# The sums of squares of four heads, taken by two reduced-form matmuls of a high and a low part

## The reference

```python
f = lbf + (1.0 - lbf) * jax.nn.sigmoid(fz)
log_f = jnp.log(f); k = 1.0 - f
o_hg = hgrn2_chunkwise(silu(q), log_f, k, i)       # per head: scores with decays, and a carried state
o_hg = rmsnorm(o_hg, hg_norm).reshape(B, T, HG_WIDTH) * jax.nn.silu(g)
o_cv = rmsnorm(gb * causal_dwconv3(gc * u), conv_norm)
return jnp.concatenate([o_hg, o_cv], axis=-1) @ w_out
```

## Time and profile before

| | us |
|---|---|
| median of 3 runs | 1118.38 |
| lowest, highest | 1118.32, 1120.45 |
| the profiled execution, its own time | 1120.16 |
| its span in the trace | 1118.2 |
| TensorE busy | 1106.8 |
| VectorE, ScalarE, GpSimd busy | 626.9, 522.2, 437.1 |

### The profile page before, as it was taken

The page is one execution under the profiler, slowest core; times in us unless marked ns, Lnnn a source line. Parts: engine busy times, 40 slices in busy tenths (PEclk is TensorE's granted clock), DMA queues, the critical chain, the costliest instruction groups (busy, mean ns, idle before and its releaser), DMA issues.

```text
span 1118.2 us, 17287 instructions
## 1 busy us (share of the span) xinstructions
PE 1106.8 (99%) x6358; PEld 971.0 (87%) x6358; DVE 626.9 (56%) x911; ACT 522.2 (47%) x725; POOL 437.1 (39%) x544
## 2 busy tenths in 40 slices
PE   9999999999999999999999999999999999999997
PEld 7889999988888888888888888888889999988886
DVE  6887777441222668888567123464787777440012
ACT  6545555542323555654466443354455555542221
POOL 0000000486665544434548883173000000485651
PEclk9999999999999999999999999999999999999999
DMA  7276775332323221222313442122187675332312
GB/s 240 76 210 188 194 197 169 114 112 96 113 94 111 77 76 57 76 76 76 113 57 133 163 157 76 39 81 102 45 226 188 178 197 169 114 113 96 112 57 76
DMA packets 48626, 135.33 MB, mean 121 GB/s; under 512 B 4672, under 2 KB 10944, under 8 KB 48448
## 3 DMA queue, kind: packets, MB, share of 16 engines
q1 hardware_dynamic: 43344, 118.38, 30.2%
q0 software_dynamic: 4032, 14.68, 7.7%
q10 hardware_dynamic: 1200, 1.57, 0.4%
HBM read 132.52 MB, written 2.10 MB: 120 GB/s over the span
## 4 chain that ended last, share of the span: by engine, by line
PE 53%; POOL 25%; issue 21%; DVE 0%; POOLq 0%; DMA 0%; ACT 0%; DVEq 0%; SPq 0%; ACTq 0%
POOL wl L438 25%; PE bank L1420 9%; PE bank L1422 9%; PE bank L1421 9%; PE bank L1522 4%; PE bank L1524 4%; PE bank L1523 4%; PE score L1523 3%; PE score L1522 3%; PE score L1524 3%; PE o_bank L1522 1%; PE o_bank L1524 1%; PE o_bank L1523 1%; PE bank L1479 1%; PE bank L1483 1%
## 5 line engine op out<-in xcount | busy, mean ns | idle before, releaser
L438 POOL TENSOR_TENSOR wl<-raw,wh 128x256 fp32r<-128x256 f32 x512 | 412.5, 839 | 326.0 <-ACT wh L472 281.8
L472 ACT ACTIVATE wh<-raw 128x1024 fp32r<-128x1024 f32 x124 | 130.1, 1054 | 162.2 <-PE bank L1422 158.1
L1420 PE MATMUL bank<-xh,wh 128*128 128x512 f32 x488 | 194.8, 399 | 0.0
L1422 PE MATMUL bank<-xh,wl 128*128 128x512 f32 x488 | 190.4, 390 | 0.0
L1421 PE MATMUL bank<-xl,wh 128*128 128x512 f32 x488 | 190.1, 390 | 0.0
L452 POOL DMA_DIRECT2D raw<-w_all x28 | 24.3, 869 | 330.1 <-DMA raw<-w_all 330.1
L1420 PE MATMUL bank<-zr,wh 128*128 128x512 f32 (+1 forms) x374 | 142.6, 381 | 0.0
L1422 PE MATMUL bank<-zr,wl 128*128 128x512 f32 (+1 forms) x374 | 141.7, 379 | 0.0
L1421 PE MATMUL bank<-zr,wh 128*128 128x512 f32 (+1 forms) x374 | 140.5, 376 | 0.0
L902 DVE SCALAR_TENSOR_TENSOR x<-bank,x 128x512 f32<-128x512 f32 (+1 forms) x31 | 21.3, 687 | 175.4 <-PE bank L1422 175.4
L1421 PEld LDWEIGHTS bank<-xl,wh 128*128 128x128 f32 x488 | 91.8, 188 | 19.9 <-issue 1.7
(11 more groups left out here) (304 smaller groups left out, 2493.8 us busy)
## 6 DMA issues: line engine op xcount, KB each, us to landing
raw<-w_all SPq DMA_DIRECT2D x200, 512.0 KB, 3.3
raw<-w_all POOLq DMA_DIRECT2D x28, 512.0 KB, 5.2
zf<-w_all SPq DMA_DIRECT2D x28, 256.0 KB, 4.5
x<-x_t SPq DMA_DIRECT2D x8, 256.0 KB, 6.2
out_t<-x SPq DMA_DIRECT2D x8, 256.0 KB, 2.4
raw<-w_all SPq DMA_DIRECT2D x6, 256.0 KB, 6.1
memf<-mem_t ACTq DMA_DIRECT2D x1, 1024.0 KB, 4.8
raw<-w_all ACTq DMA_DIRECT2D x2, 256.0 KB, 3.9
```

The costliest lines, as they stand in the source:

```text
L438: ins = nc.gpsimd.tensor_tensor(wl[:, slot, two], raw[:, slot, two], wh[:, slot, two].bitcast(f32), SUB)
L472: nc.scalar.activation(wh[:, slot, :], raw[:, slot, :], ACT.Copy).then_inc(hi_ready, 1)
L1420: nc.tensor.matmul(out_, a[0], b_[0], start=first, stop=False)
L1422: return nc.tensor.matmul(out_, a[1], b_[0], start=False, stop=last)
```

## The change

The matrix of ones gets a copy of type fp32r. In O, ScalarE copies osq to osq_h of type fp32r right after it made it. In each slot with an N step VectorE takes osq_l = osq - osq_h, as the first instruction of the slot, ahead of the eviction of the slot's projection. In N, TensorE waits for osq_lo instead of osq_ready, and for ones_ready, and makes two fp32r matmuls, ones_r by osq_h and ones_r by osq_l, into the same bank. osq_l lies in the memory of osq and osq_h in that of onrm: so osq_l is written in place, and osq_h only after the head before has released onrm (the wait for cat_lo).

```diff
--- before.py
+++ after.py
@@ -129,6 +129,7 @@
         convV, lf = ubuf[:, 0, :], ubuf[:, 1, :]
         half_tanh = gbuf[:, 0, :]
         ones = sb("ones", [128, 128])
+        ones_r = sb("ones_r", [128, 128], f32r)
         ident = sb("ident", [128, 128])
         masks = sb("masks", [128, MASK_COLS], u8)
         par = sb("par", [128, NPAR])
@@ -178,8 +179,12 @@
         kd = sb("kd", [128, T], f32, mix_mem)
         kdT = sb("kdT", [128, TT, 128], f32, mix_mem)
         S = sb("S", [128, NCH - 1, 128], f32, mix_mem)
-        osq = sb("osq", [128, T], f32, mix_mem)
-        onrm = sb("onrm", [128, T], f32, mix_mem)[:, :]
+        o_mem = ExitStack()
+        osq = sb("osq", [128, T], f32, o_mem)
+        onrm = sb("onrm", [128, T], f32, o_mem)[:, :]
+        o_mem.close()
+        osq_l = sb("osq_l", [128, T], f32r, mix_mem)
+        osq_h = sb("osq_h", [128, T], f32r, mix_mem)
         convC = sb("convC", [128, T], f32, mix_mem)
         convU = sb("convU", [128, 2 + T], f32, mix_mem)
         convO = sb("convO", [128, CC, T], f32, mix_mem)
@@ -289,6 +294,9 @@
         a22_loaded = [sem(f"a22_loaded{i}") for i in range(2)]
         x_old = sem("x_old")
         xn_new = sem("xn_new")
+        osq_hi = sem("osq_hi")
+        osq_lo = sem("osq_lo")
+        ones_ready = sem("ones_ready")
         xn_hi = sem("xn_hi")
         xn_lo = sem("xn_lo")
         t_new = sem("t_new")
@@ -730,6 +738,10 @@
                 if kind == "O":
                     act.wait_ge(o_done, h + 1)
                     nc.scalar.activation(osq[:, :], o_bank[:, :], ACT.Square).then_inc(osq_ready, 1)
+                    act.wait_ge(osq_ready, h + 1)
+                    if h > 0:
+                        act.wait_ge(cat_lo, h)
+                    nc.scalar.activation(osq_h[:, :], osq[:, :], ACT.Copy).then_inc(osq_hi, 1)
                 if kind == "N":
                     inverse_root(("N", h), osq[:, :], n_bank[:, :], 128)
                     act.wait_ge(cat_new, h + 1)
@@ -843,6 +855,8 @@
             V_ = nc.vector
             V_.memset(ones[:, :], 1.0).then_inc(consts_ready, 1)
             V_.memset(one, 1.0).then_inc(consts_ready, 1)
+            dve.wait_ge(consts_ready, 1)
+            V_.tensor_copy(ones_r[:, :], ones[:, :]).then_inc(ones_ready, 1)
             V_.memset(eps, EPS).then_inc(consts_ready, 1)
             link(V_.memset(acc[:, :], 0.0))
             V_.memset(rstd[:, :], 0.0).then_inc(group_read, 4)
@@ -1268,6 +1282,10 @@
                         .then_inc(cat_lo, 1)
 
             for at, (kind, c) in enumerate(MIX_SLOTS):
+                for step_kind, h, _ in STEPS[at]:
+                    if step_kind == "N":
+                        dve.wait_ge(osq_hi, h + 1)
+                        V_.tensor_tensor(osq_l[:, :], osq[:, :], osq_h[:, :].bitcast(f32), SUB).then_inc(osq_lo, 1)
                 g = SLOT_GROUP[at]
                 src = bank[g % 4][:, :]
                 if kind in "qfg":
@@ -1694,9 +1712,11 @@
                                                 start=False, stop=(c == NCH - 1), skip_group_check=True)
                     last.then_inc(o_done, 1)
                 if kind == "N":
-                    pe.wait_ge(osq_ready, h + 1)
+                    pe.wait_ge(osq_lo, h + 1)
                     n_wait(("N", h))
-                    nc.tensor.matmul(n_bank[:, :], ones[:, :], osq[:, :], start=True, stop=True).then_inc(n_done, 1)
+                    pe.wait_ge(ones_ready, 1)
+                    nc.tensor.matmul(n_bank[:, :], ones_r[:, :], osq_h[:, :], start=True, stop=False)
+                    nc.tensor.matmul(n_bank[:, :], ones_r[:, :], osq_l[:, :], start=False, stop=True).then_inc(n_done, 1)
 
             for at, (kind, c) in enumerate(MIX_SLOTS):
                 u = U_MIX + at
```

## The result

| | before | changed |
|---|---|---|
| median of 6 runs, us | 1118.58 | 1123.71 |
| lowest, highest | 1118.32, 1120.45 | 1122.50, 1125.01 |
| span of the profiled execution | 1118.2 | 1120.7 |
| granted TensorE clock, mean | 0.999 | 0.996 |

The account below looks back on a forecast made before the run. TensorE was taken as the bound, busy 1106.8 of 1118.2 us. Heads 0 to 3 gave 1.6 + 0.1 + 0.6 - 0.4 = +1.9 us, from a median of 1118.38 to 1120.3 us; 8-in-10 range 1117.3 to 1122.3.

Parts of the forecast that it names:

- head 0's term of the sum: Slot 9: the low part delays VectorE's chain to the factors by 1.6 us, TensorE's saving is eaten; net +1.6 us.
- three signs that were to show the prediction wrong: Slot 11's stall growing under 1 us, TensorE waiting for osq_lo, or stalls made good later, after 544 us.
- head 1: Slots 14 and 15: ScalarE's copy and the low part delay VectorE, waiting before the eviction absorbs most; net +0.1 us.
- head 2: Slot 20: the low part adds 0.61 us and the weight load at 515.75 already waits; net +0.6 us.
- head 3: Slot 25: VectorE's 3.17 us of idle time hides the low part; net -0.4 us, bounds -0.4 and 0.
- The upper bound of the recorded sum: Top of the range given by the bounds of the four heads' parts, +0.7 to +2.7 us.
- What TensorE saves: In N, the float32 sum costs 0.85 us and the new pair 0.46; 0.39 us saved a head, 1.6 in four.
- Head 0's extra 0.9 us from GpSimd's stretch: Slot 9: more VectorE differences fall into GpSimd's stretch and slow, lasting up to 0.96 us instead of 0.42.
- TensorE keeps what it saves: Rival: the low part goes into VectorE's idle time everywhere, only the 1.6 us saving shows, 1116.8 us; 14%.
- the port costs nothing more: Rival: head 0 costs only 0.6 us, total +0.9, 1119.3 us; 12%.
- Slower: Rival: ScalarE's copy ahead of slot 14's exponentials makes VectorE 0.5 us late at the eviction; 1120.7 to 1121.8 us; 28%.

Follow-up runs that it names:

- r12: The changed kernel run once more, unaltered; ratio 1.0039 to the kernel before.
- r11: The changed kernel with matmuls whose result nothing reads on TensorE, nine in slot 11 and three in slot 19; ratio 1.0016 to the kernel before.
- r2: The changed kernel with the new form in head 3 only, the other heads keeping the float32 sum; ratio 0.9992 to the kernel before.
- r5: The changed kernel with the old float32 sum on TensorE; copy and low part still made, low part unused in its own memory; ratio 1.0049 to before.
- r6: The changed kernel with head 0's low part behind slot 9's first pair of differences instead of ahead of the eviction; ratio 1.0013 to before.
- r3: The changed kernel with nine matmuls whose result nothing reads on TensorE in slot 11; ratio 1.0018 to the kernel before.
- r9: The changed kernel with the new form in heads 1 to 3, head 0 keeping the float32 sum; ratio 1.0004 to the kernel before.
- r1: The changed kernel with the new form in head 0 only, heads 1 to 3 keeping the float32 sum; ratio 1.0036 to the kernel before.
- r4: The kernel before with the square written straight as fp32r and summed by one fp32r matmul, no low part; ratio 1.0009 to before.
- r10: The kernel before with one fp32r sum, no low part, plus unread matmuls, four in slot 11 and three in slot 19; ratio 0.9990 to before.
- r7: The kernel before with the N steps' parts on ScalarE and VectorE one slot later; ratio 1.0060 to before.
- r8: The changed kernel with the N steps' parts on ScalarE and VectorE one slot later; ratio 1.0066 to the kernel before.

## Why the prediction was wrong

- **The step that failed is head 0's term of the sum.** "TensorE's 0.39 us is eaten by its longer stall at 437.96. Net +1.6" counted a stop of TensorE at its length alone. The stall was forecast at "about 2.8 us" and came at 2.67; what it does to the clock, 1.6 us behind slot 11 and as much again there or behind slot 19, had no term, and no rival had it. The total was +1.9 forecast, +4.2 measured in A (+4.8 in r12); the time lay above the range (1122.3) for this reason. None of the three signs that were to show the prediction wrong came: slot 11's stall grew by 1.9 us, TensorE never waited for osq_lo, and behind 544 us nothing changed its length. The list of signs had the same gap as the sum.
- **Without the clock the sum holds.** r11, where nothing falls, is the changed kernel with its parts showing: +1.72 us over before. By slots it has +1.48 for head 0 (forecast 1.6), +0.06 up to slot 19 for head 1 (0.1), +0.60 from there to slot 21 for head 2 (0.6), -0.42 for head 3 (-0.4). The upper bound of the recorded sum was added up wrongly: +2.7 takes head 3 at -0.4; with its own bound of 0 the parts give +3.1, still under what was measured.
- **What TensorE saves**: forecast 0.39 us a head, measured 0.41 behind head 0 and 0.40 behind head 3 (r2: 0.37). That it counts at head 3 alone is shown by r2 and r5.
- **Head 0's extra 0.9 us from GpSimd's stretch**: right, as the slot 9 rows show. r6 confirms that the place in GpSimd's stretch makes the difference, with a smaller saving (0.34 us) than the 0.6 I gave it. No run took GpSimd's stretch itself away.
- **Head 2** was right in size, yet not to be seen in the changed kernel's profile: TensorE was late by the clock and found the factors ready. r3, r9 and r11 bring it out.
- **The rivals**: "TensorE keeps what it saves" fell with r5; "the port costs nothing more" with r6. "Slower" was true in its sign and false in its mechanism: in r9 VectorE starts slot 15's eviction 0.08 us later than before, counted from the first sum, where 0.1 was forecast. No row then at hand showed a fall, so the 32% for slower could not have counted it; with the price that r3 and r6 put on such a stop, slower was by far the likeliest.

What stays open: why a stall of 0.96 to 0.99 us in slot 19 was followed by a fall in two profiles (changed kernel, r5) and not in the others with the same stall. In both a fall had come behind slot 11; in r1, r4 and r12 one had come as well, and nothing followed in slot 19. The granted clock of each execution says how much clock was lost, not where; so how often the fall behind slot 19 comes is not known. Two of 67 executions of the kernel before read 0.997, so a rare fall in it can't be excluded.

## What to carry to other kernels

A saving on the engine that is busy all the time counts only up to the next place where it already waits; look for the places with a little waiting, or none to spare, behind each edit, and ask which engine gets the new work in front of them. A stop of TensorE can cost more than its length, since the clock may fall behind it, so a delay that grows one stop from 0.8 to 2.7 us needs a second price beside its length, and splitting or filling the stop gets that part back. Of the versions that keep the low part, two are not distinguishable from before in their runs, r9 and r2, and only r2, which has the new form just where VectorE is idle, is shorter in A, by 0.4 us; r10, which leaves the low part out, is the one kernel whose interval lies under 1.

## What was not expected of the hardware

- In the profiled executions TensorE's clock fell behind stalls of 1.42, 2.28, 2.67, 2.69 and 2.69 us in slot 11 and of 1.65 and 1.83 us in slot 19. Behind 0.96 to 0.99 us in slot 19 it did both. It stayed up behind all shorter ones, but also behind 0.99 us in slot 11 and 1.09 us in slot 9 (r6), behind 1.38 and 1.41 us that follow each other closely (r7, r8), and once behind 2.8 us ahead of the second sum (r7), where r8 had a fall. So the length of one stop alone does not decide it.
- At 1.2 GHz it stayed for some 3.4 us (1.6 us lost), in r12 some 6.8 us (3.2 us lost), by the windows' readings, while TensorE was busy all along.
- A fall can hide another delay: head 2's 0.6 us vanished in the 1.6 us of the second one.
